# The delta layer's block inverse: the transpose of P squared by VectorE's 32x32 block transpose instead of a second product on TensorE

## The chip, the cores and the metric

One NeuronCore of a Trainium2 chip runs the whole program; there is no other core in play. The metric is the device time of one launch in microseconds, taken as the median of three runs. All data are fp32.

## The reference, cut to what matters

The kernel computes one inference step of two layers on 1024 prompt tokens and 8 x 16 sample tokens. Layer 0 (a linear recurrence beside windowed attention) is not touched. Layer 1 is a gated delta rule with 8 heads, in chunks of 64 tokens. Its costly piece is the inverse of a unit lower triangular matrix per chunk, which the reference does by repeated squaring:

```
def unit_lower_inverse(a, n):
    t = jnp.broadcast_to(jnp.eye(n, dtype=a.dtype), a.shape)
    p = -a
    n_steps = (n - 1).bit_length()
    for step in range(n_steps):
        t = t + jnp.matmul(t, p)
        if step + 1 < n_steps:
            p = jnp.matmul(p, p)
    return t
...
    a_mat = jnp.einsum('nbhid,nbhjd->nbhij', k_beta, kc) * decay_strict
    t_mat = unit_lower_inverse(a_mat, cb)
    w = jnp.matmul(t_mat, k_beta * jnp.exp(gcum)[..., None])
    u = jnp.matmul(t_mat, vc * bc[..., None])
```

After that a scan over the chunks carries the state, and an output projection and a norm close the layer.

## The kernel before, in words

The tokens stand in 9 tiles of 128 (`NT = 9`; 8 of the prompt, one of the samples). Each engine has its own straight list of instructions, written out by Python loops over the heads (`h`) with nothing left to run time; semaphores tie the lists together. So the order on each engine is the order in the source, and an instruction that waits holds back everything behind it on its engine.

Layer 1 runs head by head. On each engine `head(h)` is `rest(h)` (the inverse and the Gram products), then `scan(h)` (eight steps of the state), then the front of head h+1. Between the small steps of a head, TensorE fills its time with pieces of the input projection of the next head, an order written out by hand: `fill(h, p, ahead)` issues slot p, three or so units of a Strassen-like product (128x128 weights, 288 columns). ScalarE and VectorE have a `between(h, p, ahead)` at the same slots: VectorE adds finished products (L2503 to L2523), applies the taps of the convolution (L2536, L2547, in head 0 also L2425) and the gates (L2553, L2560). The last head has no next one (`ahead` is false) and fills with parts of the output projection (512 columns) instead.

The inverse is made on the 32x32 diagonal blocks first: each tile has four of them, one per strip of 32 partitions, so all blocks of a head fill a buffer of 128 partitions x (9 x 32) columns. `PW` holds P, `YT0` the growing sum, and `PTc` (two buffers) P transposed. A matmul gives lhsT transposed times rhs, so P squared needs P transposed as the stationary side. `rest` has five rounds. In rounds 1 to 4 TensorE first makes the transpose of P squared into PSUM bank 7, 36 matmuls of 32x32 (4 strips x 9 tiles), called W product below:

```
x = mm(B(7)[q, 32 * k:32 * k + 32], PW[q, k], turned[q, k], start=True, stop=True)
```

and then 36 matmuls into bank 5 (the last tile in bank 6): P squared in round 1, P squared and P times the sum side by side in rounds 2 and 3 (32x64), the sum alone in round 4 and 5. Called N product below. ScalarE copies bank 7 into `PTc[:, r % 2]` (L1899) and counts `w_ev`; VectorE takes bank 5 in `power(h, r)` (L2667, L2672, L2674, L2678, L2680) and counts `n_ev1`. Round r+1 on TensorE waits for both. Two slots of fill and other products (`extra`) lie between two rounds.

For the first round VectorE already makes the transpose itself: `front(h)` builds P (L2605 to L2617) and calls `dve.transpose` on the 128x288 buffer (L2618), which turns each 32x32 block; `x0_ready` lets round 1 go. Another such transpose (L2682) stands at the end of round 5.

Two more things matter for the steps below. After round 1 VectorE does `outputs(h - 1, 2)` (L2731), which waits for transposes on TensorE (L935) and whose semaphore `y1_done` TensorE waits for before it transposes the next four tiles (`extra(1)`, L935). And VectorE's next addition of a projection product (L2523) frees the bank in which TensorE starts slot 2. L932 and L935 are the helper lines through which all matmuls and all transposes of TensorE are issued; L48 is the helper of most waits. GpSimd runs small sums, in head 0 a long one (L852, 128x2304).

Of the kernel before, what the change touches and what calls it, by code (L numbers as in the profile page):

```python
# [18 lines left out]
ALU = mybir.AluOpType  # L19
ACT = mybir.ActivationFunctionType  # L20
# [6 lines left out]
NT = SEQ // P + 1  # L27
# [4 lines left out]
H = 8  # L32
# [12 lines left out]
def wait(eng, sem, value):  # L45


    eng.wait_ge(sem, value)  # L48
    if not isinstance(value, int):
        eng.sem_inc(PASSED[eng.engine], 1)  # L50


PASSED = {}

# [146 lines left out]
class Count:  # L203
# [17 lines left out]
    def sync(self):  # L221

        wait(self.eng, *self.last)
# [27 lines left out]
def encoder(nc, I, O):  # L251
    ctx = ExitStack()
    with ctx:  # L253
        sem_made = {}

        def sem(name):
            if name not in sem_made:
                sem_made[name] = ctx.enter_context(nc.semaphore(name))
            return sem_made[name]
# [126 lines left out]
        XZPY, Wc = take(4, NT, 32), take(NT, 32)  # L386
        XT0, YT0, PW = XZPY[:, 0], XZPY[:, 3], XZPY[:, 2]
        PTc = take(2, NT, 32)
# [46 lines left out]
        B = lambda b: psum[:, b, :]  # L435

        @block.sync
        def _(sp):
            PASSED[sp.engine] = sem("sp_passed")
            for ap, name in ((ident, "ident"), (cT, "cT"), (npre, "npre")):  # L440
                sp.dma_start(ap, I[name]).then_inc(sem("const_in"), 16)

# [148 lines left out]
            for q in range(4):  # L591
                r = slice(32 * q, 32 * q + 32)
# [89 lines left out]

            head(H - 1, 0)
            sp.wait_ge(sem("eq_ready"), 3 * H)
            sp.wait_ge(sem("w_ev"), 6 * H)
            residual(0)
            for i, t in enumerate(OUT_ORDER[:-1]):
                residual(i + 1)
# [12 lines left out]
        @block.gpsimd  # L701
        def _(pool):
            c = Count(pool, sem("pool_own"))
            PASSED[pool.engine] = sem("pool_passed")
            c.mark(pool.memset(halfneg, -0.5))
            c.sync()

# [219 lines left out]

        @block.tensor
        def _(pe):
            PASSED[pe.engine] = sem("pe_passed")  # L930
            def mm(*a, **k):
                return pe.matmul(*a, **k)  # L932

# [454 lines left out]
            def rest(h, ahead):  # L1388
                first = isinstance(h, int) and h == 0
                lo, hi = range(4), range(4, 8)  # L1390
                L = 6 * h

                def extra(n):

# [31 lines left out]
                for r in range(1, 6):  # L1426
                    if r == 1:
                        pe.wait_ge(sem("x0_ready"), h + 1)
                        if not first:
                            pe.wait_ge(sem("o_ready"), 8 * h)  # L1430
                    else:
                        pe.wait_ge(sem("n_ev1"), 7 * h + r - 1)
                        pe.wait_ge(sem("w_ev"), L + r - 1)
                    if r == 2:
                        pe.wait_ge(sem("ssq_ready"), h + 1)
                    turned = PTc[:, (r - 1) % 2]
                    if r < 5:
                        for k in range(NT):
                            for q in strips:
                                x = mm(B(7)[q, 32 * k:32 * k + 32], PW[q, k], turned[q, k], start=True, stop=True)  # L1440
                        x.then_inc(sem("w_mm"), 1)
                    for k in range(NT if r < 5 else NT - 1):
                        for q in strips:
                            if r in (2, 3):
                                o = B(5)[q, 64 * k:64 * k + 64] if k < 8 else B(6)[q, 0:64]
                                x = mm(o.rearrange("p (a t) -> p a t", a=2), turned[q, k], XZPY[q, 2:4, k],
                                       start=True, stop=True)
                            else:
                                x = mm(B(5)[q, 32 * k:32 * k + 32], turned[q, k], PW[q, k] if r == 1 else YT0[q, k],
                                       start=True, stop=True)  # L1450
                    x.then_inc(sem("n_mm"), 1)
                    fill(h, 2 * r - 2, ahead)
                    extra(2 * r - 2)
                    if r == 1 and first:
                        gram_q(0)
                    if r < 5:
                        fill(h, 2 * r - 1, ahead)
                        extra(2 * r - 1)
# [6 lines left out]
                               XT0[a:a + 32, k], start=True, stop=True)  # L1465
                x.then_inc(sem("w_mm"), 1)
                fill(h, 9, ahead)
                pe.wait_ge(sem("w_ev"), L + 5)
                for k in range(NT - 1):
                    r = slice(32, 64)  # L1470
                    mm(B(6)[r, 32 * k:32 * k + 32], YT0[r, k], Wc[r, k], start=True, stop=True)
                    for a in (0, 64):
                        r = slice(a + 32, a + 64)
# [8 lines left out]
                    x = mm(B(5)[low, 64 * k:64 * k + 64], UM[top, k, low], XW[top, k], start=True, stop=True)  # L1482
                x.then_inc(sem("w_mm"), 1)
                fill(h, 11, ahead)
                wait(pe, sem("w_ev"), L + 6)
                wait(pe, sem("diag_ready"), 2 * h + 2)
                wait(pe, sem("y5_ev"), h + 1)
                for k in range(NT - 1):
# [110 lines left out]
        @block.scalar  # L1599
        def _(act):  # L1600
            c = Count(act, sem("act_own"))
            PASSED[act.engine] = sem("act_passed")
            wait(act, sem("const_in"), 48)
            act.activation(ctmp, cT, ACT.Tanh, scale=0.5).then_inc(sem("act_step"), 1)

# [57 lines left out]
            for m in range(2):  # L1663
                for n in range(3):
# [4 lines left out]
                    else:  # L1669
                        r = SEQ - 2 * NC  # L1670
# [214 lines left out]
            def scaled_ee(h, lo, hi):  # L1885

                if lo == 0:
                    wait(act, sem("um_ready"), h + 1)
                    wait(act, sem("eec_ready"), h + 1)
                for k in range(lo, hi):  # L1890
                    i = act.activation(EE[:, k], EE[:, k], ACT.Copy, scale=r2[:, k:k + 1])
                if hi == NT:
                    i.then_inc(sem("ee_ready"), 1)

            def rest(h, ahead):
                L = 6 * h
                for r in range(1, 5):
                    wait(act, sem("w_mm"), L + r)
                    act.activation(PTc[:, r % 2].rearrange("p c t -> p (c t)"), B(7)[:, 0:32 * NT], ACT.Copy  # L1899
                                   ).then_inc(sem("w_ev"), 1)  # L1900
                    if r == 1:
                        scaled_ee(h, 4, NT)
                    between(h, 2 * r - 2, ahead)
                    between(h, 2 * r - 1, ahead)
                between(h, 8, ahead)
                wait(act, sem("w_mm"), L + 5)
                act.activation(Wc[:, 0:NT - 1].rearrange("p c t -> p (c t)"), B(5)[:, 0:32 * (NT - 1)], ACT.Copy
                               ).then_inc(sem("w_ev"), 1)
                between(h, 9, ahead)
                wait(act, sem("n_mm"), 7 * h + 6)  # L1910
                for a in (0, 64):
                    i = act.activation(YF[a:a + 32, 0:NT - 1, a + 32:a + 64],
                                       B(7)[a:a + 32, 0:256].rearrange("p (c t) -> p c t", t=32),
                                       ACT.Copy, scale=-1.0)
                i.then_inc(sem("y5_ev"), 1)
                between(h, 10, ahead)
                wait(act, sem("w_mm"), L + 6)
                act.activation(XW[64:128].rearrange("p c t -> p (c t)"), B(5)[64:128], ACT.Copy
                               ).then_inc(sem("w_ev"), 1)
                between(h, 11, ahead)  # L1920
                between(h, 12, ahead)
# [100 lines left out]
        @block.vector  # L2022
        def _(dve):
            c = Count(dve, sem("dve_own"))
            PASSED[dve.engine] = sem("dve_passed")
            def mod_zero():
                c.mark(dve.memset(modb, 0.0))
                dve.memset(sel, 0.0).then_inc(sem("dve_step"), 1)
# [446 lines left out]
            flat = lambda a: a.rearrange("p a t -> p (a t)")  # L2475
# [181 lines left out]
            def upper(h, n):  # L2657
                dve.wait_ge(sem("gram_mm"), 2 * h + n + 1)
                dve.tensor_tensor(UM[:, 4 * n:4 * n + 4], four(2 + n), EE[:, 4 * n:4 * n + 4], ALU.mult
                                  ).then_inc(sem("umf_ready"), 1)  # L2660

            def power(h, r):

                dve.wait_ge(sem("n_mm"), 7 * h + r)
                b5 = B(5)[:, 0:32 * NT].rearrange("p (c t) -> p c t", t=32)
                if r == 1:
                    c.tell(dve.tensor_copy(PW, b5), sem("n_ev1"), 7 * h + 1)  # L2667
                    return
                dve.wait_ge(sem("x0_ready" if r == 2 else "n_ev1"), h + 1 if r == 2 else 7 * h + r - 1)
                if r < 4:  # L2670
                    turn = lambda a: a.rearrange("p h c t -> p c h t")
                    dve.tensor_tensor(XZPY[:, 2:4, 8], XZPY[:, 1:4:2, 8],  # L2672
                                      B(6)[:, 0:64].rearrange("p (h t) -> p h t", h=2), ALU.add)
                    dve.tensor_tensor(turn(XZPY[:, 2:4, 0:8]), turn(XZPY[:, 1:4:2, 0:8]),  # L2674
                                      B(5).rearrange("p (c h t) -> p c h t", h=2, t=32), ALU.add
                                      ).then_inc(sem("n_ev1"), 1)
                elif r == 4:
                    dve.tensor_tensor(YT0, YT0, b5, ALU.add).then_inc(sem("n_ev1"), 1)  # L2678
                else:
                    c.mark(dve.tensor_tensor(YT0[:, 0:NT - 1], YT0[:, 0:NT - 1], b5[:, 0:NT - 1], ALU.add))  # L2680
                    c.sync()
                    dve.transpose(flat(XT0), flat(YT0)).then_inc(sem("n_ev1"), 1)  # L2682
# [324 lines left out]
```

## Time and profile before

| | us |
|---|---|
| median of 3 runs | 1406.89 |
| lowest and highest | 1403.92 and 1408.66 |
| the profiled execution, span from first to last instruction | 1401.9 |
| TensorE busy | 1360.5 |
| VectorE busy | 809.7 |
| ScalarE busy | 438.9 |
| GpSimd busy | 264.2 |

The profile tells the span of its execution and no other time of it; the median of the timed runs is 5.0 us longer than that span. Layer 1's heads run from about 606 us to about 1290 us of the span, some 87.5 us for each head. The granted clock of TensorE is 1.00 in each head (0.999 in the mean over the span). An fp32 matmul of the program appears as two matmul and two weight-load records.

To read it: TensorE's busy share is near 100% through all heads, so the first question is who could make TensorE wait, and the second is in which stretch its own list gets shorter.

### The profile page before, as it was taken

How to read it: one execution, taken by the hardware profiler on the slowest of the kernel's cores; microseconds unless marked ns; L12 is line 12 of the kernel's file. 1: busy time of each engine (PE TensorE's matmuls, PEld its weight loads, DVE VectorE, ACT ScalarE, POOL GpSimd, SP SyncE). 2: the span in 40 equal slices, each digit the busy share in tenths (PEclk: the TensorE clock that was granted, in tenths of full speed). 3: DMA queues.
4: the chain of work that ended last, by engine and by line, in shares of the span. 5: the costliest groups of instructions: out<-in, count | busy, mean ns of one | idle time of the engine just before them, and what ended most of it. 6: DMA issues, size and time to landing. Idle time of an engine off the chain costs nothing.

```text
span 1401.9 us, 30739 instructions
## 1 busy us (share of the span) xinstructions
PE 1360.5 (97%) x12976; PEld 930.0 (66%) x12976; DVE 809.7 (58%) x1834; ACT 438.9 (31%) x1062; POOL 264.2 (19%) x402
## 2 busy tenths in 40 slices
PE   5999999999999999999999999999999999989998
PEld 3577765666653454567887787777777778865543
DVE  4747772444432253676876848768486685862244
ACT  4114441444430222521433323233232331422211
POOL 1113200000000110533322323123231332210111
PEclk9999999999999999999999999999999999999999
DMA  9610108000055411111112021020120201430133
GB/s 371 235 45 27 38 0 329 1 1 1 3 220 209 148 40 60 29 63 35 63 34 66 34 60 70 33 66 35 44 86 33 67 34 42 144 123 25 47 120 120
DMA packets 56317, 112.16 MB, mean 80 GB/s; under 512 B 34698, under 2 KB 37586, under 8 KB 53346
## 3 DMA queue, kind: packets, MB, share of 16 engines
q1 hardware_dynamic: 56180, 110.21, 22.8%
q8 instruction: 102, 1.67, 0.5%
q14 instruction: 35, 0.29, 0.1%
HBM read 91.79 MB, written 18.40 MB: 79 GB/s over the span
## 4 chain that ended last, share of the span: by engine, by line
PE 68%; issue 1%; DVE 1%; ACT 0%; DVEq 0%; POOLq 0%; POOL 0%; ACTq 0%
PE psum L932 66%; PE psum L935 2%; DVE mem L2425 0%; DVE mem L2627 0%; DVE mem L2422 0%; DVE mem L2857 0%; DVEq L253 0%; ACT mem L1882 0%; ACT mem L2019 0%; DVE mem L2674 0%; POOLq L253 0%; DVE mem L2553 0%; ACT mem L1794 0%; DVE mem L2635 0%; DVE mem L2358 0%
## 5 line engine op out<-in xcount | busy, mean ns | idle before, releaser
L932 PE MATMUL psum<-mem 32*32 32x32 f32 (+11 forms) x12368 | 1299.7, 290 | 20.5 <-issue 10.0
L932 PEld LDWEIGHTS psum<-mem 32*32 32x32 f32 (+5 forms) x12368 | 861.1, 137 | 424.2 <-issue 230.5
L2536 DVE SCALAR_TENSOR_TENSOR mem<-mem 128x576 f32<-128x576 f32 (+1 forms) x126 | 106.4, 844 | 0.0
L935 PE MATMUL psum<-mem 128*128 128x128 f32 (+1 forms) x608 | 85.9, 278 | 15.1 <-ACT mem L1622 11.3
L935 PEld LDWEIGHTS psum<-mem 128*128 128x128 f32 (+1 forms) x608 | 71.3, 144 | 41.1 <-issue 25.6
L762 POOL TENSOR_SCALAR mem<-mem 128x1 f32<-128x1 f32 x17 | 3.6, 213 | 343.9 <-ACT mem L1765 343.9
L1929 ACT ACTIVATE mem<-mem 128x128 f32<-128x128 f32 x72 | 22.0, 305 | 127.7 <-DVE mem L2779 74.5
L2378 DVE SCALAR_TENSOR_TENSOR mem<-psum,mem 128x1024 f32<-128x1024 f32 x12 | 15.2, 1270 | 60.4 <-POOL mem L764 60.4
L1744 ACT ACTIVATE mem<-mem 128x256 f32<-128x256 f32 x72 | 35.5, 494 | 46.4 <-DVE mem L2338 46.4
L1765 ACT ACTIVATE mem<-psum 128x1024 f32<-128x1024 f32 x12 | 12.3, 1024 | 110.5 <-PE psum L932 108.7
L2078 DVE TENSOR_SCALAR mem<-psum,mem 128x128 f32<-128x128 f32 x64 | 21.1, 404 | 39.1 <-PE psum L935 39.1
L1827 ACT ACTIVATE mem<-mem 128x576 f32<-128x576 f32 (+1 forms) x42 | 32.7, 779 | 28.1 <-DVE mem L2514 28.1
L2328 DVE CUSTOM_DVE_ANT_0 mem<-psum,mem 128x256 f32<-128x256 f32 x72 | 25.6, 421 | 23.7 <-PE psum L932 23.7
L1817 ACT ACTIVATE mem<-psum 128x288 f32<-128x288 f32 x28 | 11.4, 406 | 85.9 <-PE psum L932 85.9
L1856 ACT ACTIVATE mem<-mem 128x1176 f32<-128x1176 f32 x24 | 28.3, 1178 | 30.5 <-DVE mem L2536 26.5
L829 POOL COPY mem<-mem 128x3 f32<-128x3 f32 x24 | 8.4, 349 | 151.8 <-DVE mem L2494 70.9
L2560 DVE SCALAR_TENSOR_TENSOR mem<-mem 128x1024 f32<-128x1024 f32 (+1 forms) x31 | 35.9, 1158 | 1.9 <-ACT mem L1856 1.8
L803 POOL TENSOR_TENSOR mem<-mem 128x512 f32<-128x512 f32 x14 | 15.2, 1089 | 112.6 <-issue 108.1
L1899 ACT ACTIVATE mem<-psum 128x288 f32<-128x288 f32 x32 | 13.1, 410 | 70.0 <-PE psum L932 69.9
L2740 DVE SCALAR_TENSOR_TENSOR mem<-psum,mem 128x128 f32<-128x128 f32 x56 | 19.4, 347 | 25.4 <-PE psum L932 25.4
L2756 DVE COPY mem<-psum 128x128 f32<-128x128 f32 x64 | 18.5, 288 | 21.0 <-PE psum L932 20.9
L2771 DVE SCALAR_TENSOR_TENSOR mem<-mem,psum 128x128 f32<-128x128 f32 x56 | 19.3, 344 | 17.1 <-PE psum L932 17.1
(242 smaller groups left out, 1188.7 us busy)
## 6 DMA issues: line engine op xcount, KB each, us to landing
mem<-modw SPq DMA_DIRECT2D x12, 2048.0 KB, 13.5
mem<-w SPq DMA_DIRECT2D x44, 512.0 KB, 4.1
mem<-x SPq DMA_DIRECT2D x1, 4608.0 KB, 18.0
x_dram<-mem SPq DMA_DIRECT2D x9, 512.0 KB, 2.6
mem<-row_dram SPq DMA_DIRECT2D x8, 576.0 KB, 5.0
mem<-x_dram SPq DMA_DIRECT2D x9, 512.0 KB, 3.6
mem<-wout SPq DMA_DIRECT2D x4, 1024.0 KB, 8.4
mem<-gs SPq DMA_DIRECT2D x8, 512.0 KB, 3.3
```

Source lines behind the costliest of these rows:

```text
L932: return pe.matmul(*a, **k)
L935: return pe.transpose(out, in_, ident[0:n, 0:n])
L1744: c.mark(act.activation(SS[:, a], SS[:, a], ACT.Exp, scale=HD ** -0.5, bias=nm[:, a:a + 1], accum_out=den[:, a:a + 1]))
L1827: act.activation(CV[:, m, lo:hi], U1[:, m, lo:hi], ACT.Copy, scale=CW[:, 3 * g + ORDER[m], 0:1]).then_inc(sem("pj_ev"), 1)
L1856: act.activation(U1[:, m, PRE:], CV[:, m, 0:UC], ACT.Tanh, scale=0.5).then_inc(sem("th1"), 1)
L1929: x = act.activation(SQJ, OO[:, k], ACT.Square, accum_out=sso[:, k:k + 1])
L2078: i = dve.tensor_scalar(HT[:, k, bass.ds(t * P, P)], src[k], modT[:, KT + k, 0:1], modT[:, k, 0:1], ALU.mult, ALU.add)
L2328: i = dve.tensor_tensor_reduce(SS[:, n], B(bk)[:, a * 256:(a + 1) * 256], mask, 1.0, -3.0e38, ALU.add, ALU.max, mx[:, n:n + 1])
L2536: x = dve.scalar_tensor_tensor(cvm, U1[:, m, lo + j:hi + j], CW[:, 3 * g + ORDER[m], j:j + 1], cvm, ALU.mult, ALU.add)
L2560: dve.scalar_tensor_tensor(S1[:, m, a:b], T[:, a:b], 1.0, CV[:, m, a:b], ALU.add, ALU.mult)
L2740: dve.scalar_tensor_tensor(RR, at_(6, 0), HC[:, 1, k:k + 1], VB[:, k], ALU.mult, ALU.add).then_inc(sem("r_ready"), 1)
L2771: dve.scalar_tensor_tensor(SP, SP, EG[:, bass.ds(h, 1), k], at_(6, 2), ALU.mult, ALU.add).then_inc(sem("st_ready"), 1)
```

## The change

In rounds 1 to 3 the W product on TensorE and ScalarE's copy of bank 7 are gone. VectorE, once it has written P squared to `PW` in `power(h, r)`, waits for its own write and transposes `PW` block by block into `PTc[:, r % 2]`, and counts a new semaphore `turned`. Round r+1 on TensorE waits for `turned` instead of `n_ev1` and `w_ev`. Round 4, in which P squared itself is no longer made, keeps the W product and ScalarE's copy; the wait for `o_ready`, which guards bank 7, moves from round 1 to round 4. `w_mm` and `w_ev` count 3 a head instead of 6. A counter (`PASSED`) that only waits on a value held in a register would raise is taken out.

```diff
@@ on TensorE, rest
                     if r == 1:
                         pe.wait_ge(sem("x0_ready"), h + 1)
-                        if not first:
-                            pe.wait_ge(sem("o_ready"), 8 * h)
+                    elif r < 5:
+                        pe.wait_ge(sem("turned"), 3 * h + r - 1)
                     else:
-                        pe.wait_ge(sem("n_ev1"), 7 * h + r - 1)
-                        pe.wait_ge(sem("w_ev"), L + r - 1)
+                        pe.wait_ge(sem("n_ev1"), 7 * h + 4)
+                        pe.wait_ge(sem("w_ev"), L + 1)
                     if r == 2:
                         pe.wait_ge(sem("ssq_ready"), h + 1)
                     turned = PTc[:, (r - 1) % 2]
-                    if r < 5:
+                    if r == 4:
+                        if not first:
+                            pe.wait_ge(sem("o_ready"), 8 * h)
                         for k in range(NT):
                             for q in strips:
                                 x = mm(B(7)[q, 32 * k:32 * k + 32], PW[q, k], turned[q, k], start=True, stop=True)
@@ on ScalarE, rest
                 for r in range(1, 5):
-                    wait(act, sem("w_mm"), L + r)
-                    act.activation(PTc[:, r % 2].rearrange("p c t -> p (c t)"), B(7)[:, 0:32 * NT], ACT.Copy
-                                   ).then_inc(sem("w_ev"), 1)
                     if r == 1:
                         scaled_ee(h, 4, NT)
+                    elif r == 4:
+                        wait(act, sem("w_mm"), L + 1)
+                        act.activation(PTc[:, 0].rearrange("p c t -> p (c t)"), B(7)[:, 0:32 * NT], ACT.Copy
+                                       ).then_inc(sem("w_ev"), 1)
@@ on VectorE
+            def turned(h, r):
+                c.sync()
+                dve.transpose(flat(PTc[:, r % 2]), flat(PW)).then_inc(sem("turned"), 1)
+
             def power(h, r):
...
                 if r == 1:
                     c.tell(dve.tensor_copy(PW, b5), sem("n_ev1"), 7 * h + 1)
+                    turned(h, 1)
                     return
...
-                    dve.tensor_tensor(turn(XZPY[:, 2:4, 0:8]), turn(XZPY[:, 1:4:2, 0:8]),
-                                      B(5).rearrange("p (c h t) -> p c h t", h=2, t=32), ALU.add
-                                      ).then_inc(sem("n_ev1"), 1)
+                    c.tell(dve.tensor_tensor(turn(XZPY[:, 2:4, 0:8]), turn(XZPY[:, 1:4:2, 0:8]),
+                                             B(5).rearrange("p (c h t) -> p c h t", h=2, t=32), ALU.add),
+                           sem("n_ev1"), 7 * h + r)
+                    turned(h, r)
```

## Rows read from the trace of the kernel before

**Rows 1.** The page: busy time of each engine, and the chain that ended last
```profile
PE 1360.5 (97%) x12976; PEld 930.0 (66%) x12976; DVE 809.7 (58%) x1834; ACT 438.9 (31%) x1062; POOL 264.2 (19%) x402
...
PE 68%; issue 1%; DVE 1%; ACT 0%; DVEq 0%; POOLq 0%; POOL 0%; ACTq 0%
```
**Rows 2.** Waits of TensorE from 600 to 1290 us: total, times, longest
```profile
PE psum L932 <- issue: 10.0, 11, 1.5
PE psum L932 <- DVE mem L2553: 0.7, 1, 0.7
```
**Rows 3.** Stretches (us, busy by engine, clock, DMA), round 1 to round 4's start
```profile
794.47:813.78 19.31, 19.05 (x511) 16.30 (x510) 13.96 (x25) 5.73 (x13) 1.44 (x3) 1.00 0.02 4
...
1056.65:1078.30 21.65, 19.36 (x511) 16.50 (x510) 13.96 (x25) 5.73 (x13) 1.43 (x3) 1.00 0.02 3
...
1233.64:1255.80 22.16, 18.11 (x499) 14.28 (x498) 13.70 (x26) 5.02 (x11) 0.16 (x1) 1.00 0.38 140
sum 142.21, PE 132.91 PEld 112.60 DVE 97.42 ACT 39.37 POOL 8.75; mean PE 18.99 PEld 16.09 DVE 13.92 ACT 5.62 POOL 1.25
...
618.14:639.88 21.74, 21.03 (x579) 16.69 (x578) 20.83 (x30) 6.61 (x17) 10.94 (x8) 1.00 0.02 4
```
**Rows 4.** Stretches: one undisturbed round 1, 2 and 3, and their sum
```profile
794.47:800.06 5.59, 5.59 (x168) 4.70 (x167) 5.03 (x11) 2.44 (x7) 0.35 (x2) 1.00 0.01 3
1152.84:1159.50 6.66, 6.66 (x174) 5.82 (x173) 5.28 (x10) 1.20 (x3) 0.00 (x0) 1.00 0.01 2
807.13:813.78 6.65, 6.65 (x173) 5.81 (x172) 3.66 (x5) 2.10 (x4) 1.09 (x1) 1.00 0.01 2
sum 18.90, PE 18.90 PEld 16.32 DVE 13.97 ACT 5.73 POOL 1.44; mean PE 6.30 PEld 5.44 DVE 4.66 ACT 1.91 POOL 0.48
```
**Rows 5.** Stretches: one W product; between two stops, of 256 and of 512 instructions
```profile
800.04:800.66 0.62, 0.62 (x71) 0.60 (x72) 0.62 (x2) 0.00 (x0) 0.00 (x0) 1.00 0.14 26
...
1058.82:1065.78 6.96, 5.54 (x126) 4.49 (x127) 4.61 (x8) 1.55 (x4) 0.00 (x0) 1.00 0.01 2
1242.93:1250.14 7.21, 6.08 (x256) 5.49 (x255) 3.50 (x7) 2.58 (x4) 0.00 (x0) 1.00 0.03 9
```
**Rows 6.** Groups of TensorE by shape in 1233.6:1255.8 (head 7): busy, mean ns, idle
```profile
L932 PE MATMUL psum<-mem 32*32 32x32 f32 x288 | 3.5, 194 | 2.9 <-issue 2.9
L932 PE MATMUL psum<-mem 32*32 32x64 f32 x144 | 2.7, 215 | 1.1 <-issue 1.1
```
**Rows 7.** Order of time, TensorE, a stop in head 4's round 4
```profile
990.57 0.65 PE L932 MATMUL psum<-mem 128*128 128x288 f32 x2 [0.75 <-issue]
```
**Rows 8.** The page, DMA queues: packets, MB, share
```profile
q8 instruction: 102, 1.67, 0.5%
```
**Rows 9.** Order of time, VectorE after round 1 of head 2; TensorE there
```profile
797.50 0.45 DVE L2667 COPY mem<-psum 128x288 f32<-128x288 f32 x1
798.05 0.75 DVE L2731 SCALAR_TENSOR_TENSOR mem<-psum,mem 128x512 f32<-128x512 f32 x1
...
797.41 0.60 PE L935 MATMUL psum<-mem 128*128 128x128 f32 x4
...
799.31 0.60 PE L935 MATMUL psum<-mem 128*128 128x128 f32 x4
```
**Rows 10.** All of two lines: duration ns min/median/max, first and last start
```profile
L2618 DVE STREAM_TRANSPOSE mem<-mem x8: 470/471/472, 612.4 to 1231.2; 128x288 f32<-128x288 f32 x8
...
L1899 ACT ACTIVATE mem<-psum x32: 392/410/412, 619.8 to 1256.7; 128x288 f32<-128x288 f32 x32
```
**Rows 11.** Order of time, head 0, VectorE and GpSimd
```profile
628.14 6.00 DVE L2425 SCALAR_TENSOR_TENSOR mem<-mem 128x384 f32<-128x384 f32 x2
...
634.40 0.54 DVE L2553 SCALAR_TENSOR_TENSOR mem<-mem,psum 128x384 f32<-128x384 f32 x1
...
635.47 0.63 DVE L2425 SCALAR_TENSOR_TENSOR mem<-mem 128x408 f32<-128x408 f32 x1
...
628.66 5.06 POOL L852 TENSOR_TENSOR mem<-mem 128x2304 f32<-128x2304 f32 x1 [3.57 <-PE psum L932]
```

More of the change, by code:

```diff
@@ L48, in wait @@
     eng.wait_ge(sem, value)
-    if not isinstance(value, int):
-        eng.sem_inc(PASSED[eng.engine], 1)
-PASSED = {}
 TURN_BANK = (6, 7, 5, 6)
@@ L438, in _ @@
         def _(sp):
-            PASSED[sp.engine] = sem("sp_passed")
             for ap, name in ((ident, "ident"), (cT, "cT"), (npre, "npre")):
@@ L684, in _ @@
             sp.wait_ge(sem("eq_ready"), 3 * H)
-            sp.wait_ge(sem("w_ev"), 6 * H)
+            sp.wait_ge(sem("w_ev"), 3 * H)
             residual(0)
@@ L703, in _ @@
             c = Count(pool, sem("pool_own"))
-            PASSED[pool.engine] = sem("pool_passed")
             c.mark(pool.memset(halfneg, -0.5))
@@ L929, in _ @@
         def _(pe):
-            PASSED[pe.engine] = sem("pe_passed")
             def mm(*a, **k):
@@ L1390, in rest @@
                 lo, hi = range(4), range(4, 8)
-                L = 6 * h
+                L = 3 * h
                 def extra(n):
@@ L1467, in rest @@
                 fill(h, 9, ahead)
-                pe.wait_ge(sem("w_ev"), L + 5)
+                pe.wait_ge(sem("w_ev"), L + 2)
                 for k in range(NT - 1):
@@ L1484, in rest @@
                 fill(h, 11, ahead)
-                wait(pe, sem("w_ev"), L + 6)
+                wait(pe, sem("w_ev"), L + 3)
                 wait(pe, sem("diag_ready"), 2 * h + 2)
@@ L1601, in _ @@
             c = Count(act, sem("act_own"))
-            PASSED[act.engine] = sem("act_passed")
             wait(act, sem("const_in"), 48)
@@ L1895, in rest @@
             def rest(h, ahead):
-                L = 6 * h
+                L = 3 * h
                 for r in range(1, 5):
-                    wait(act, sem("w_mm"), L + r)
-                    act.activation(PTc[:, r % 2].rearrange("p c t -> p (c t)"), B(7)[:, 0:32 * NT], ACT.Copy
-                                   ).then_inc(sem("w_ev"), 1)
                     if r == 1:
                         scaled_ee(h, 4, NT)
+                    elif r == 4:
+                        wait(act, sem("w_mm"), L + 1)
+                        act.activation(PTc[:, 0].rearrange("p c t -> p (c t)"), B(7)[:, 0:32 * NT], ACT.Copy
+                                       ).then_inc(sem("w_ev"), 1)
                     between(h, 2 * r - 2, ahead)
@@ L1905, in rest @@
                 between(h, 8, ahead)
-                wait(act, sem("w_mm"), L + 5)
+                wait(act, sem("w_mm"), L + 2)
                 act.activation(Wc[:, 0:NT - 1].rearrange("p c t -> p (c t)"), B(5)[:, 0:32 * (NT - 1)], ACT.Copy
@@ L1916, in rest @@
                 between(h, 10, ahead)
-                wait(act, sem("w_mm"), L + 6)
+                wait(act, sem("w_mm"), L + 3)
                 act.activation(XW[64:128].rearrange("p c t -> p (c t)"), B(5)[64:128], ACT.Copy
@@ L2024, in _ @@
             c = Count(dve, sem("dve_own"))
-            PASSED[dve.engine] = sem("dve_passed")
             def mod_zero():
```

## The prediction

> **What bounds the kernel now.** I read the page's busy times and chain first: TensorE is busy 97% of the span and holds 68% of the chain that ended last, nobody else over 1% [rows 1]. So time is saved only where TensorE's own list gets shorter or its stops go. Next, its waits through layer 1's heads: in 690 us it stands still 10.7 us, of which one wait of 0.7 is for VectorE and 11 stops, 10.0 us, are for "issue", that is for nothing the profile knows [rows 2]. Then the stretches from the start of round 1 to the start of round 4, which hold all that the change edits: the same 511 matmul records take 19.3 us in head 2 and 21.7 in head 5 [rows 3]; three rounds in which nothing stops are 18.90 [rows 4]. The stops lie in or just behind the small matmuls: in head 7 4.0 us before 32x32 and 32x64 ones [rows 6], in head 4 0.75 behind round 4 [rows 7]. Last, VectorE: 14 us busy of such 19 in heads 1 to 7, but 20.8 of 21.7 in head 0 [rows 3].
>
> **What the stops are.** From one stop's end to the next TensorE runs 126 matmuls and 127 weight loads, between two others 256 and 255 [rows 5]: with the few semaphore instructions, which these counts leave out, that is one and two times 256 instructions, and other pairs of stops that I counted are whole multiples too. The instruction queue moved 1.67 MB in 102 packets, 16.4 KB each [rows 8]; 2 x 12976 instructions [rows 1] over 102 is 254. So instructions come in blocks of 256, and TensorE stops at a block's edge when it ran through the block faster than the next arrived. A block that stopped had taken 1.3 to 2.4 us without its stop, in two cases 5.3 (its fetch began late); blocks that took over 3.5 us nearly never did. Rounds 1 to 3 are where blocks are fast: W product and N product together are 288 instructions in 1.4 to 1.8 us.
> The Trainium skill, "Runtime: NRT & Kernel Launch", section "Instruction fetch mechanics", also has blocks of 256 instructions, but says the fetch is hidden since the sequencer dispatches slower than the memory fills, and that TensorE's store holds 2048 of them. The trace speaks against that part; it comes back as a rival.
>
> **The change part by part.**
> *W product, 3 x 8 removed.* One is 72 matmul records, 0.62 us [rows 5]: TensorE's list is shorter by 24 x 0.62 = 14.9 us.
> *Stops.* With 144 instructions where 288 were, a block in rounds 2 and 3 holds one burst and slow fill on both sides and takes 5 to 8 us. I counted the blocks forward through the shortened list (144 fewer per W product, and two semaphore instructions fewer a head): where 14 stops lay (the 11 and three of under 0.2 us), five short blocks are left, three in round 4 (heads 1, 3, 5; that round is not edited) and two in round 1 (heads 5, 7), where gram_q's matmuls stand close before.
> *ScalarE's copy, 24 x 0.41 us [rows 10].* ScalarE is busy 31% [rows 1]; nothing. The cover is its own idle time, and without it TensorE would have had 0.41 less latency per round.
> *VectorE's transpose, 24 added.* The same instruction on the same shape takes 0.47 us [rows 10]; with the wait for its own write some 0.50. Nothing could make it cheaper than 0.47, since this is its time from memory to memory on this very buffer; dearer it can be: it could be held up while GpSimd works, where a VectorE operation took 5.4 us (two took 6.00, a usual one 0.63) [rows 11]. I take 0.50 and keep both ends. What waits for it: TensorE's next round, which starts 5.6 to 6.7 us after the last one [rows 4], while VectorE had P squared 2.1 us before round 2 in head 2 (797.95 and 800.06) [rows 4, 9] and longer before in the other rounds; so that wait costs nothing. What is queued behind it is the point.
> *Behind the transpose of round 1.* In head 2 VectorE's copy ends at 797.95, is late because of work before it and does not move when TensorE gets faster. L2731 starts at 798.05, when the transposes (797.41 + 0.60) are there, and ends at 798.80; TensorE needs it at 799.31 [rows 9]. After: 797.95 + 0.50 + 0.75 = 799.2, while TensorE now comes at 799.31 - 0.62 = 798.69. So it waits 0.5, and of round 1's 0.62 only 0.1 is left. The copy ends 3.5 us after round 1's start in each of heads 1 to 7, so I take this for all seven.
> *Behind round 2's.* VectorE is 0.1 late or less at L2523, which frees the bank of slot 2: 0.5 us over seven heads, my estimate. Round 3: VectorE has idle time of over 2 us; nothing.
> *Head 0.* VectorE is full, and the wait of 0.7 stands at the end of round 3 [rows 2]. L852 on GpSimd, started by TensorE, holds VectorE's L2425 until 633.7 [rows 11]. The transposes of rounds 1 and 2 push 1.0 us of VectorE's work; some of it, the second transpose itself among it, falls into the 5 us in which L2425 would have been held anyway, so 0.5 stays at L2553 and 0.5 more behind round 3's. TensorE, which waits for L2553 and then L2659, gets nothing for its three W products and ends 1.0 us later than before. If the transpose is held as L2425 is, 2.0 later.
> The Trainium skill, "GPSIMD Engine Reference", section "8. Key points", says that contention with GpSimd is for VectorE instructions with two SBUF inputs or in a 2-port mode. The one that was held has two SBUF inputs, which agrees; the transpose has one, so by that rule it is not held and the loss is 1.0, against 2.0 without the rule. No run here shows a transpose beside GpSimd.
> *The rest.* `o_ready` moves behind three rounds, it was there long before: 0. `PASSED` never counts, as all values are constants: 0. SyncE's wait means the same event.
>
> **The sum**, on the profiled execution. Heads 1 to 7 take 142.2 us in this stretch [rows 3]. After, heads 1 to 6 take 18.90 [rows 4] - 0.1 - 0.62 - 0.62 = 17.56 each, 105.4. Head 7: 22.16 less its three stops, 4.0 idle [rows 6] and 3 x 0.19 by which the last matmul before each is drawn longer, 17.6; less 1.34, 16.2. Together 121.6: 20.6 gained, 9.2 of it by list and 11.4 by stops. Round 4's stop in head 4, 0.75 + 0.19 [rows 7], goes: 0.9. New stops: three in round 4 at 0.8, two in round 1 at 1.0, of which 0.45 each lies beside TensorE's wait for L2731: 3.5 lost. Slot 2: 0.5. Head 0: 1.0. In all 20.6 + 0.9 - 3.5 - 0.5 - 1.0 = 16.5. After round 4 nothing is changed and each engine's work follows TensorE, so it is kept to the end. 1401.9 - 16.5 = 1385.4 for the span; the median of the runs is 5.0 longer, 1390.4.
>
> **The rivals.**
> *A. The stops stay* (they are a cost per block or have another cause, as the page's rule of a hidden fetch would have it): the gain is the list's alone, 9.2 - 0.5 - 1.0 = 7.7, 1399.2. For it: the number of blocks falls by only 14 in 102. Against: all stops are in fast blocks. By the page's rule the time would be this one.
> *B. More comes.* No new stops (3.5), VectorE's round 1 chain gives way since a shorter wait lets its other work slip, and head 0 loses nothing: up to 14.9 + 12.1 (the 11 stops with 0.19 each) = 27.0, 1379.9. Against it: VectorE's copy has no idle time before it.
> *C. Slower: VectorE becomes the bound of rounds 1 to 3 in every head.* Then each head gets longer by its three transposes, 1.5 us, whatever TensorE saves: 12.2 in all, 1419. It decides where VectorE has less than 1.5 + 1.9 us free in the stretch. Head 0 has 0.9 and is such a case; heads 1 to 7 have 5.3 and more [rows 3]. A transpose held by GpSimd in them as well would bring them nearer, but GpSimd is busy only 1.4 us of such a stretch. A milder form, in which the late work of VectorE meets waits of the scan that I did not look at and eats 12 to 16 us, ends at no change.
> *D. It does not do what it says*, for instance by a transpose that turns something else: the same instruction makes round 1's operand already, so I leave it at nothing.
>
> **How the numbers follow.** Forecast 0.58, A 0.22, B 0.10, C in its mild form 0.06 and in full 0.04. About 0.3%, 4.2 us, is what a measurement of this kernel can tell from no change. The forecast, B and nearly all of A are faster: 0.89. Same: the mild C and a bit of A, 0.07; slower: 0.04. Likeliest 1390.4, its own range 1386 to 1395; the range for 8 in 10 takes in A and most of B, 1383 to 1400.
>
> **What would show it.** TensorE 1728 matmul records fewer, in all heads; its stops for issue 10 down to about 3 us, none in rounds 2 and 3. The stretch of round 1 to 4 at 17.6 us in heads 1 to 6, 22.7 in head 0. A new wait of TensorE for L2731 (its line shifts with the edit), some 0.4 us in each of seven heads, in round 1, and a longer one for the gate in head 0. 32 transposes of 0.47 us beside the 8 at the end of round 5, none much longer. ScalarE's copies 8 instead of 32. I am wrong if stops remain in rounds 2 and 3, if TensorE waits for `turned`, or if a transpose takes microseconds.

## The result, and the profile after

The changed kernel takes 1385.03 us (median of 4 runs, 1383.95 to 1386.51), the kernel before 1406.86 beside it (4 runs, 1403.92 to 1408.66): a ratio of 0.9848, 95% interval 0.9834 to 0.9862, so 1.5% or 21.8 us faster. The forecast was 1390.4, its range 1383 to 1400. In the profiled executions the span went from 1401.9 to 1384.7 us, where 1385.4 was forecast. One further execution of the kernel before, among the 17 beside e5 to e7, took 2823.69 us, twice the others, at a full clock; it stands in no ratio.

The page of the kernel after: busy times, the instruction queue and the chain, as in [rows 1, 8].

```profile
PE 1346.1 (97%) x11248; PEld 914.7 (66%) x11248; DVE 819.6 (59%) x1858; ACT 430.4 (31%) x1038; POOL 264.5 (19%) x402
...
q8 instruction: 89, 1.46, 0.4%
...
PE 63%; DVE 6%; issue 1%; ACT 0%; DVEq 0%; POOLq 0%; POOL 0%; ACTq 0%
```

1728 matmuls and as many weight loads are gone, 24 ScalarE copies too, and 24 VectorE instructions have come. There are 13 fetches fewer. VectorE's share of the chain went from 1 to 6%: the chain now runs through it somewhere, and the waits say where.

The waits of TensorE in the same stretch as [rows 2] (600 to 1290 us), kernel after: total, times, longest.

```profile
PE psum L924 <- DVE mem L2546: 2.2, 1, 2.2
PE psum L927 <- DVE mem L2731: 2.1, 7, 0.3
PE psum L924 <- DVE mem L2632: 1.9, 1, 1.9
PE psum L924 <- issue: 0.8, 1, 0.8
```

Of 11 stops for issue (10.0 us) one is left (0.8). Waits for VectorE stand in their place: seven short ones for L2731, as forecast, and two long ones in head 0, for L2546 (the gate, L2553 before) and for L2632, the last step before round 2 may start.

The stretches from round 1's start to round 4's, kernel after, answering to [rows 3] (columns as there): head 0, head 2, head 5, head 7.

```profile
618.78:643.50 24.72, 20.62 (x363) 15.91 (x362) 23.66 (x33) 5.62 (x14) 10.76 (x8) 0.93 0.01 2
...
796.20:813.74 17.54, 17.23 (x295) 14.36 (x294) 14.95 (x28) 3.77 (x8) 1.44 (x3) 1.00 0.01 2
...
1051.55:1069.09 17.54, 17.23 (x296) 14.36 (x295) 14.94 (x28) 3.77 (x8) 1.43 (x3) 1.00 0.01 2
...
1222.61:1238.68 16.07, 15.82 (x283) 12.08 (x283) 14.59 (x29) 3.18 (x6) 0.17 (x1) 1.00 0.51 192
```

Heads 1 to 6 now all take 17.54 us (19.3 to 21.6 before), and head 7 takes 16.07. Heads 1 to 7 together: 121.3, where 142.21 was. Head 0 went the other way: 24.72 instead of 21.74, with VectorE busy 23.66 of it and the granted clock at 0.93; the lower clock is 1.7 us of the 3.0 lost, as the part on the clock works out.

VectorE and TensorE after round 1 of head 2 in order of time (start, us, then the group), kernel after, as [rows 9].

```profile
799.22 0.45 DVE L2665 COPY mem<-psum 128x288 f32<-128x288 f32 x1
799.71 0.48 DVE L2658 STREAM_TRANSPOSE mem<-mem 128x288 f32<-128x288 f32 x1
800.11 0.71 DVE L2731 SCALAR_TENSOR_TENSOR mem<-psum,mem 128x512 f32<-128x512 f32 x1
...
800.88 0.66 PE L927 MATMUL psum<-mem 128*128 128x128 f32 x4 [0.31 <-DVE mem L2731]
```

The transpose is in front of L2731, and TensorE stands 0.31 us for L2731 before its next transposes.

Head 0 in order of time, kernel after: VectorE, and under it two of GpSimd's instructions.

```profile
621.17 0.48 DVE L2658 STREAM_TRANSPOSE mem<-mem 128x288 f32<-128x288 f32 x1
621.57 1.31 DVE L2415 TENSOR_SCALAR mem<-mem 128x384 f32<-128x384 f32 x1
...
629.90 0.48 DVE L2658 STREAM_TRANSPOSE mem<-mem 128x288 f32<-128x288 f32 x1
...
630.48 5.61 DVE L2418 SCALAR_TENSOR_TENSOR mem<-mem 128x384 f32<-128x384 f32 x2
...
636.34 0.55 DVE L2546 SCALAR_TENSOR_TENSOR mem<-mem,psum 128x384 f32<-128x384 f32 x1
...
621.38 1.28 POOL L785 TENSOR_TENSOR mem<-mem 128x512 f32<-128x512 f32 x1
...
629.95 5.06 POOL L845 TENSOR_TENSOR mem<-mem 128x2304 f32<-128x2304 f32 x1 [4.40 <-PE psum L924]
```

Two things are to be seen. The second transpose starts 0.05 us ahead of GpSimd's 5 us and runs beside them, and it still takes 0.48, while the products of the taps around it (L2418) are held as before. And the first transpose has pushed L2415 into GpSimd's sum at L785: it takes 1.31 us, where it takes 0.46 at the same place in a kernel without the transpose (below).

All transposes of the inverse, kernel after: duration ns min/median/max, first and last start.

```profile
L2658 DVE STREAM_TRANSPOSE mem<-mem x24: 478/479/480, 621.2 to 1234.3; 128x288 f32<-128x288 f32 x24
```

### The profile page after: what moved, and what is told of

It is laid out like the page before. It is cut to its first block, busy times and chain, and to the rows that moved or that the text cites. A ratio compares the mean times of both kernels' runs of the same rounds, so it can differ in the third digit from the quotient of the medians.

```text
span 1384.7 us, 27267 instructions
## 1 busy us (share of the span) xinstructions
PE 1346.1 (97%) x11248; PEld 914.7 (66%) x11248; DVE 819.6 (59%) x1858; ACT 430.4 (31%) x1038; POOL 264.5 (19%) x402
## 4 chain that ended last, share of the span: by engine, by line
PE 63%; DVE 6%; issue 1%; ACT 0%; DVEq 0%; POOLq 0%; POOL 0%; ACTq 0%
PE psum L924 61%; PE psum L927 2%; DVE mem L2529 1%; DVE mem L2418 1%; DVE mem L2620 1%; DVE mem L2731 0%; DVE mem L2509 0%; DVE mem L2628 0%; DVE mem L2608 0%; DVE mem L2610 0%; DVE mem L2598 0%; DVE mem L2601 0%; DVE mem L2665 0%; DVE mem L2625 0%; DVE mem L2611 0%
## 5 line engine op out<-in xcount | busy, mean ns | idle before, releaser
L924 PE MATMUL psum<-mem 32*32 32x32 f32 (+12 forms) x10640 | 1284.0, 305 | 15.5 <-ACT mem L1746 4.5
L924 PEld LDWEIGHTS psum<-mem 128*128 128x128 f32 (+5 forms) x10640 | 846.3, 143 | 418.0 <-issue 221.6
L1810 ACT ACTIVATE mem<-psum 128x288 f32<-128x288 f32 x28 | 11.4, 408 | 101.5 <-PE psum L924 101.5
L2553 DVE SCALAR_TENSOR_TENSOR mem<-mem 128x1024 f32<-128x1024 f32 (+1 forms) x31 | 36.8, 1186 | 1.8 <-ACT mem L1849 1.8
L2771 DVE SCALAR_TENSOR_TENSOR mem<-mem,psum 128x128 f32<-128x128 f32 x56 | 19.3, 344 | 17.1 <-PE psum L924 17.1
L1603 ACT ACTIVATE mem<-mem 128x1024 f32<-128x1024 f32 x18 | 18.9, 1052 | 30.9 <-DMA mem<-x 14.6
```

Of the source, the lines that this page charges most:

```text
L2553: dve.scalar_tensor_tensor(S1[:, m, a:b], T[:, a:b], 1.0, CV[:, m, a:b], ALU.add, ALU.mult)
L2771: dve.scalar_tensor_tensor(SP, SP, EG[:, bass.ds(h, 1), k], at_(6, 2), ALU.mult, ALU.add).then_inc(sem("st_ready"), 1)
```

## The experiments

Line numbers shift by a few from kernel to kernel. A stretch is always from the first 32x32 matmul of round 1 to that of round 4. e1 to e4 ran on one chip (before: 1405.75, 9 runs), e5 to e7 on another (before: 1405.12, 17 runs). Three questions: what are the stops, what does the place of the transpose cost in heads 1 to 7, and what in head 0.

**e5: the products stay on TensorE, their result unused.** Same number of TensorE instructions as before the change, 12976.

```
+                    if r < 4:
+                        for k in range(NT):
+                            for q in strips:
+                                mm(B(7)[q, 32 * k:32 * k + 32], PW[q, k], turned[q, k], start=True, stop=True)
```

> The changed kernel, but TensorE also makes the W product in rounds 1 to 3 of each head (144 instructions, 0.62 us each), and nobody reads it. Theory (saved are the list, some 9.4 us in heads 1 to 7 since round 1 gives little and head 0 nothing, and stops for instruction blocks, some 11 us in the profile and up to 16 in the timed runs): 1385 + 9.4 + 11 to 16, 1405 to 1410, with 10 us or so of idle for issue back inside the small matmuls of rounds 1 to 3. Rival (what went was the wait for ScalarE's copy, and the stops were by chance): 1385 + 9.4, 1394.

Measured: 1409.16 us (12 runs, 1406.85 to 1410.48), ratio to before 1.0024 (1.0014 to 1.0033). Its page:

```profile
PE 1361.8 (97%) x12976; PEld 932.1 (66%) x12976; DVE 820.5 (58%) x1858; ACT 430.1 (31%) x1038; POOL 264.3 (19%) x402
...
q8 instruction: 102, 1.67, 0.5%
```

Its waits of TensorE, 600 to 1290 us:

```profile
PE psum L924 <- issue: 12.4, 12, 3.0
PE psum L924 <- DVE mem L2636: 1.3, 1, 1.3
```

The 102 fetches are back and so are the stops, 12 with 12.4 us; heads 1 to 7 take 145.85. So the whole gain hangs on the TensorE instructions that are gone. Taking ScalarE's copies away brings nothing: with VectorE's transposes in their place the kernel is 0.24% slower than before. In the profiled executions it is 5.1 us (1407.0 and 1401.9). Three losses together are a little more than that: 2.4 of longer stops (12.4 against 10.0), 1.6 in head 0 (its stretch is 23.36 against 21.74), and 1.7 by a lower clock in head 7, behind its stop of 3.0 us. That stop, and the stretch of head 7 with the clock at 0.93:

```profile
1241.62 3.90 PE L924 MATMUL psum<-mem 32*32 32x32 f32 x57 [3.05 <-issue]
...
1237.58:1260.96 23.38, 19.24 (x503) 15.19 (x502) 14.97 (x29) 3.17 (x6) 0.15 (x1) 0.93 0.31 122
```

**e6: TensorE's time kept, its instructions not.** Each W product is replaced by three 128x128x128 products of the identity: 12 instructions, weight loads included, where the W product has 144.

```
+                    if r < 4:
+                        for k in range(3):
+                            mm(at_(7, k), ident, ident, start=True, stop=True)
```

> The changed kernel, but in rounds 1 to 3 TensorE makes three 128x128x128 products of the identity in bank 7, read by nobody: 0.66 us of TensorE's time as in a W product, but 12 instructions instead of 144. Theory (stops come from running through 256 instructions faster than the next 256 arrive): the time comes back, the stops do not: 1385 + 10 = 1395, idle for issue under 2 us. Rival (stops go with TensorE's work or with bank 7, not with the number of instructions): as e5_w_kept, 1405 or more.

Measured: 1395.87 us (6 runs, 1395.19 to 1397.03), ratio 0.9929 (0.9915 to 0.9943). Waits of TensorE, 600 to 1290 us:

```profile
PE psum L924 <- DVE mem L2549: 1.3, 1, 1.3
PE psum L924 <- DVE mem L2635: 1.2, 1, 1.2
PE psum L924 <- issue: 0.5, 2, 0.3
```

The stops are down from 12.4 us to 0.5 although TensorE has work at every place where e5 has it, and the medians of e5 and e6 are 13.3 us apart. Heads 1 to 6 take 18.36 each. The substitute of round 1 stands ahead of the first 32x32 matmul, so this stretch holds only two of the three, as the count of 128x128 products shows: in head 2 (e6 first, then e2) it has 47 where the same stretch of e2 has 34; twelve are the two substitutes, and one is the last record of the third, which reaches into the stretch.

```profile
L924 PE MATMUL psum<-mem 128*128 128x128 f32 x47 | 6.2, 275 | 0.0
...
L924 PE MATMUL psum<-mem 128*128 128x128 f32 x34 | 4.6, 275 | 0.0
```

Against the 17.05 of e2 and e4, in which TensorE doesn't wait for VectorE either, two cost 1.3 us, 0.65 each, and the third lies between the stretches, which are 0.66 us a head longer than in the changed kernel (68.23 and 67.57). So a substitute costs what was expected (0.66) and no less than a W product (0.62), and TensorE's own work doesn't explain any of the distance from e5. The stops do, 11.9 us, with the clock's 1.7 in e5's head 7: the spans are 13.6 us apart (1407.0 and 1393.4). The stops come from the number of instructions.

**e7: every later instruction moved 128 places on.** Semaphore increments that nobody waits for, at the head of TensorE's list, in the changed kernel.

```
+            for _ in range(128):
+                pe.sem_inc(sem("pe_pad"), 1)
```

> The changed kernel with 128 more semaphore instructions at the very start of TensorE's list, where it waits for data anyway. Nothing else changes but where the edges of the 256-instruction blocks fall. Theory: the one stop of the changed kernel (head 5, behind round 4, 0.8 us idle) goes, and stops appear, if anywhere, in round 4 of head 2 and behind round 3 or in round 4 of heads 4 and 6; total time within 2 us of 1385. Rival (stops have their own places, by data DMAs or banks): the stop stays at head 5's round 4.

Measured: 1398.16 us (6 runs, 1394.35 to 1398.66), ratio 0.9936 (0.992 to 0.9952). The expectation of the total failed by 13 us. The increments are not free, and they don't fit into the wait for data. TensorE's first matmul, in the changed kernel and in e7:

```profile
9.68 1.94 PE L927 MATMUL psum<-mem 128*128 128x128 f32 x8 [9.68 <-ACT mem L1615]
...
22.79 3.43 PE L927 MATMUL psum<-mem 128*128 128x128 f32 x15 [22.79 <-issue]
```

In e7's trace the 128 increments start from 3.27 to 22.68 us, 0.15 us apart; the data, for which the changed kernel waits until 9.68, is there long before they end. TensorE makes up a part of that at later waits, and loses 1.7 us by a lower clock behind a wait at 256 us: round 1 of head 0 starts at 630.18 instead of 618.78, 11.4 us later. The stretches are untouched (24.70, and 121.27 for heads 1 to 7). The one stop of the changed kernel, in order of time:

```profile
1071.99 1.13 PE L924 MATMUL psum<-mem 128*128 128x288 f32 x4 [0.78 <-issue]
```

And one of the two of e7:

```profile
1169.07 0.27 PE L927 MATMUL psum<-mem 128*128 128x128 f32 x1
1169.87 0.55 PE L927 MATMUL psum<-mem 128*128 128x128 f32 x3 [0.53 <-issue]
```

At the old place, head 5's round 4, e7 doesn't stop (TensorE runs through there without idle time); this stop is in head 6, and the other, of 0.3 us, is in round 4 of head 4; head 2, the third place that was named, has none. I numbered TensorE's matmul and weight load records and its semaphore instructions in the traces of all kernels: each stop for issue of 0.2 us and more in layer 1's heads comes just ahead of a record with the same remainder modulo 256 (193, counted from 0), in e7 too. That is what a block's edge would do; a property of the instruction that comes late would not move with the count.

**e1: head 0 keeps the old scheme** (W product on TensorE, ScalarE's copy), heads 1 to 7 the new one.

```
+                    elif first and r < 5:
+                        pe.wait_ge(sem("n_ev1"), r - 1)
+                        pe.wait_ge(sem("w_ev"), r - 1)
...
+                    if h == 0 and r < 4:
+                        wait(act, sem("w_mm"), r)
+                        act.activation(PTc[:, r % 2].rearrange("p c t -> p (c t)"), B(7)[:, 0:32 * NT], ACT.Copy
```

> The changed kernel, but head 0 keeps the W product and ScalarE's copy in rounds 1 to 3; heads 1 to 7 as changed. Theory (head 0 is VectorE's: its two first transposes push 1 us of VectorE work, and a TENSOR_SCALAR into GpSimd's way, so that the stretch from round 1 to round 4 took 24.7 us there against 21.7 before): the stretch falls back to 21.5 to 21.9, 3.0 us faster than the changed kernel, 1382.0. Rival (the 3 us are chance, of GpSimd's or the DMAs' timing in that execution): 1384 to 1386, no difference.

Measured: 1382.76 us (5 runs, 1381.62 to 1383.62), ratio 0.984 (0.9821 to 0.9858); span 1381.0, 3.7 under the changed kernel's. Waits of TensorE, 600 to 1290 us:

```profile
PE psum L927 <- DVE mem L2741: 2.1, 7, 0.3
PE psum L924 <- DVE mem L2554: 0.9, 1, 0.9
```

Head 0's stretch is back at 21.75, the others stay at 121.28, and the two waits of 1.9 and 2.2 are one of 0.9. So the changed kernel loses 3.0 us in head 0 in its profiled execution, although it drops three products there; what of that is the change and what the clock, e2 tells. Of the 3.7 us between the spans 0.9 is the stop of head 5, which is gone here with the moved edges. The medians are 2.3 apart, where 3.0 was expected.

**e2: the transpose of round 1 behind L2731.**

```
                     c.tell(dve.tensor_copy(PW, b5), sem("n_ev1"), 7 * h + 1)
-                    turned(h, 1)
...
                             outputs(h - 1, 2, 4, 8, 3)
+                        turned(h, 1)
```

> The changed kernel, but in round 1 of heads 1 to 7 VectorE does outputs (L2731) before the transpose instead of behind it. Theory (in round 1 TensorE waits for L2731 behind the transpose, 0.3 us idle and 0.5 us lost in each of seven heads): L2731 ends at about the time TensorE comes, 0.35 us per head gained, 2.5 in all, 1382.5, and the wait for it goes from 2.1 us in total to under 0.7. Rival (the transpose is now too late for round 2, which starts 5 us after round 1, and the wait moves there): 1385, with TensorE waiting for the transpose.

Measured: 1381.98 us (4 runs, 1380.67 to 1383.66), ratio 0.9835 (0.9815 to 0.9854); span 1380.3. Its waits of TensorE, 600 to 1290 us:

```profile
PE psum L924 <- DVE mem L2546: 2.2, 1, 2.2
PE psum L924 <- DVE mem L2632: 1.9, 1, 1.9
PE psum L924 <- issue: 0.6, 1, 0.6
```

Its stretch of head 0:

```profile
619.43:642.47 23.04, 18.96 (x364) 14.72 (x363) 22.02 (x33) 5.50 (x14) 10.74 (x8) 1.00 0.01 2
```

The seven waits for L2731 are gone and heads 1 to 6 take 17.05 each: 0.49 less, one transpose, where 0.35 was expected; 121.3 became 118.1. TensorE doesn't miss the operand, which now comes 0.5 us later after round 1's start. Head 0 gives a control that I had not planned. Its order is the same as in the changed kernel and so are its two waits, 2.2 and 1.9, but here the clock stayed at 1.00 and the stretch is 1.68 us shorter.

**e3: both.** The edits of e1 and e2 together.

> Both edits together: head 0 as before the change, and in heads 1 to 7 L2731 ahead of round 1's transpose. If the two costs are separate they add: 3.0 + 2.5 under the changed kernel, 1379.5. If one was not there, 1382 or more.

Measured: 1379.48 us (4 runs, 1378.12 to 1381.36), ratio 0.9817 (0.9797 to 0.9837); span 1378.7. Waits of TensorE, 600 to 1290 us:

```profile
PE psum L924 <- DVE mem L2554: 0.9, 1, 0.9
PE psum L924 <- issue: 0.3, 1, 0.3
```

Both gains are there: heads 1 to 7 take 118.19. It is 26.3 us under the kernel before on its chip, where the changed kernel is 21.8 under its own; its slowest run is below the changed kernel's fastest. It is the best version that I have.

**e4: neither product nor transpose.**

```
-                        pe.wait_ge(sem("turned"), 3 * h + r - 1)
+                        pe.wait_ge(sem("n_ev1"), 7 * h + r - 1)
...
-                    turned(h, r)
```

> Neither W product nor transpose in rounds 1 to 3: TensorE reads the first transpose of P again in each round (part of the computation is left out: P is not squared rightly) and waits only for P squared. It is the changed kernel without VectorE's cost. Theory (the 24 transposes cost 3.0 us in head 0 and 0.5 in each of heads 1 to 7, and nothing elsewhere): 6.6 us faster than the changed kernel, 1378.4. Rival (VectorE's additions cost nothing, the list and the stops are all): 1385.

Measured: 1381.24 us (4 runs, 1379.65 to 1381.94), ratio 0.9827 (0.9808 to 0.9846); span 1377.9. Its waits of TensorE, 600 to 1290 us:

```profile
PE psum L924 <- DVE mem L2546: 2.2, 1, 2.2
PE psum L924 <- issue: 1.0, 1, 1.0
PE psum L924 <- DVE mem L2632: 0.6, 1, 0.6
```

VectorE at L2415 in head 0, in order of time, the group that took 1.31 us in the changed kernel:

```profile
620.38 0.46 DVE L2415 TENSOR_SCALAR mem<-mem 128x384 f32<-128x384 f32 x1
```

This is what the 24 transposes cost where they stand: heads 1 to 6 take 17.05 without them, the same as e2, so behind L2731 they are free there; in head 0 the stretch is 21.77 against 24.72, and against e2's 23.04, where no clock was lost, 1.3 us less. The spans differ by 6.8 us, the timed medians only by 3.8, and the median lies between the two numbers that the expectation names. Of the 6.8, 1.7 is the changed kernel's lower clock in head 0, which e4's execution doesn't have; 5.1 is left, against 6.6 expected with 3.0 for head 0. How much of the distance between spans and medians comes from the chips, these runs don't separate.

## Why the prediction was right, and where it was not

- **Stops.** Right, and shown: e5 brings them back, e6 keeps TensorE busy without them, e7 moves them by moving the count. The Trainium skill ("Runtime: NRT & Kernel Launch", "Instruction fetch mechanics") has the fetch hidden, which would have given rival A; these rows speak against it, and agree with its blocks of 256 instructions. I had the remaining stops too high: 3.5 us for five, where one of 0.8 came; the one that came is one of the five places named (head 5, round 4). Why the other four had none, no run here tests.
- **The list and the rounds.** 17.56 us forecast for heads 1 to 6, 17.54 measured; 16.2 and 16.07 for head 7. The sum of 121.6 stands against 121.3. Its split was written as 9.2 by list and 11.4 by stops; seven times 1.34 is 9.4, so it should be 9.4 and 11.2, and rival A 1399.0.
- **L2731.** Forecast 0.5 us in each of seven heads; 2.1 in the waits, and 0.49 a head by e2, which takes away the cause. Most of the 0.2 a head between the two is overlap that the wait takes away: in e2 the transposes of TensorE start at 798.85, 0.16 us before the drawn end of the products ahead of them (797.39 + 1.62).
- **The cover.** ScalarE's copies were worth nothing, and TensorE waits for no `turned`. Slot 2 was estimated at 0.5 us; no wait shows it.
- **The transpose.** 0.479 us in all 24, also beside GpSimd (629.90 to 630.38, GpSimd from 629.95 to 635.01). The Trainium skill ("GPSIMD Engine Reference", "8. Key points") names contention for instructions with two SBUF inputs or in a 2-port mode, and the transpose, with one input, shows none. It also fits L2415: a TENSOR_SCALAR between two SBUF buffers went from 0.46 to 1.31 us beside L785, though whether it ran in a 2-port mode the trace doesn't tell.
- **Head 0.** The term that was mis-sized: "ends 1.0 us later" was forecast, 3.0 measured (21.75 to 24.72, and e1 takes them back). That VectorE is full there and the gate comes late was right. Two things were missing. First, I looked only at GpSimd's long instruction (L852 before), not at its small sums: the transpose of round 1 pushes L2415 under L785, 0.85 us more, and TensorE already waits 1.9 us for round 2's condition L2632, where it did not wait before. The stretch without a clock loss, e2's 23.04, puts this mechanism at 1.3 us. That this is near 1.0 is luck in part: the 1.0 was made of 0.5 at the gate and 0.5 behind round 3, by the transposes of rounds 1 and 2. In the traces the 1.3 is all there at round 2's condition (it ends 8.25 us after round 1's start, 6.98 before) and is the same at the gate (17.56 and 16.26, both starts); from TensorE's restart behind the gate to round 4 e2 takes 4.90 us and the kernel before 4.88, so the second and third transpose cost nothing. Second, the clock, next.
- **The clock.** Not in the prediction. Stretches around the end of the wait for L2546 in the kernel after (from the wait's end on):

```profile
636.94:640.00 3.06, 3.06 (x8) 2.27 (x9) 2.99 (x6) 0.57 (x1) 0.00 (x0) 0.56 0.00 0
640.00:642.00 2.00, 2.00 (x12) 1.83 (x11) 1.92 (x5) 0.87 (x2) 0.20 (x1) 0.82 0.00 0
```

  The granted clock is 0.56 and 0.82 of full speed. The trace's own record of it has 3.41 us at the lower level (1.2 of 2.4 GHz) from 637.31 on, and 0.44 x 3.06 + 0.18 x 2.00 = 1.7 us are lost. TensorE had stood 2.2 us just before. e2 and e4 have the same wait and no such dip, and e2's stretch is shorter by 1.68; e7 has it again. Other stops of this length behave alike: e5 has such a dip behind the stop of 3.0 us in head 7. In layer 0 all nine traces have a wait of 2.12 us at about 246 us (e7: 256 us), and in two of them, e3 and e7, the clock falls behind it, in e3 as follows:

```profile
245.69 1.21 PE L927 MATMUL psum<-mem 128*128 128x128 f32 x5 [2.12 <-DVE mem L2316]
...
245.86:249.28 3.42, 3.42 (x11) 2.52 (x10) 0.00 (x0) 0.77 (x2) 0.00 (x0) 0.50 0.01 2
```

  So a wait of over 2 us here costs its length and, in some executions, 1.7 us more. What decides it stays open.
- **From span to median.** I added 5.0 us, the distance of the profiled execution before to its median. All runs show 1.8 us between span and time of the same execution; the other 3.2 was that this execution of before was a quick one (1401.9 + 1.8 = 1403.7 against 1406.86). The profiled one of after was slower than its median (1386.5 against 1385.03). Hence 17.2 us between the spans and 21.8 between the medians: 17.2 + 3.2 + 1.5. The right forecast from the span would have been 1401.9 - 16.5 + 1.8 = 1387.2, and by the medians 1406.86 - 16.5 = 1390.4. The measured median, 1385.03, lies inside the wide range, 1383 to 1400, but 1 us below the forecast's own, 1386 to 1395: the timed medians fell by 21.8 us where 16.5 were forecast, and why the timed executions of the kernel before were so much longer than its profiled one stays open.

The parts of the 17.2: heads 1 to 7 bring 20.9; head 0 costs 3.0, its start is 0.6 later (618.14 to 618.78, ahead of any edited instruction), and what lies between the stretches costs 0.2, since the stops that went there (0.8) and the one that came (0.9) are about even. That the span was hit to 0.7 us is partly luck: 2.6 too much for new stops and 0.5 for slot 2 stood against 2.0 too little for head 0, 1.7 of it the clock, and the 0.6 of the start. Rival B's time, 1379.9, is where e3 arrives (1379.48), with what B named: no new stop of over 0.3 us, no wait behind L2731, no loss in head 0. It is not B's sum, though: e3 leaves head 0's products on TensorE, and its span is 23.2 us under that of before, where B has 27.0; the rest is the distance from span to median.

## What to carry to other kernels

Where an engine stands for "issue", count its instructions between the stops: if the distances are multiples of one number, the remedy is fewer instructions in the fast bursts, and the gain can be as large as that of the work itself (here 11 us of stops beside 10 us of TensorE's list in heads 1 to 7). An operation moved to an idle enough engine is free only behind what the bound engine is about to need: look at what is queued behind it and put it there, since one place further down was worth 0.5 us a head. Cost the one head or tile whose engine is already full apart from the others, with every instruction that it would be pushed beside; the best version here leaves that one as it was.

## What the runs showed that was not expected

- Stops for issue of 0.2 us and more in layer 1's heads occur only at one remainder modulo 256 of TensorE's instruction count, in every trace here that has them; they are up to 3.0 us long (e5, head 7). TensorE resumed 1.2 to 1.5 us after the last packet of the instruction queue had landed.
- A semaphore increment at the head of TensorE's list takes 0.15 us (e7, 128 of them), so padding moves the whole program.
- VectorE's transpose of 128x288 fp32 takes 0.48 us in the two places of head 0 where GpSimd works beside it, too, while a TENSOR_SCALAR of 128x384 went from 0.46 to 1.31 beside a GpSimd sum.
- After a wait of 2.2 us in head 0 the granted clock fell to its lower level for 3.41 us in two of four kernels that have the same wait at the same place; after a wait of 2.12 us in layer 0, in two of nine.
